# One 512-column pass of a split-precision gemm written as two passes of 256 columns

## The chip, the cores and the metric

The kernel runs on one NeuronCore of one Trainium2 chip. The metric is the device time of one execution in microseconds. A profile is one more execution, recorded by the hardware profiler.

## What is computed

Two transformer-like blocks run one after the other on one sequence of 256 tokens and a model width of 2048, all in float32. The first has a gated linear attention mixer, the second has a three-branch mixer (block attention, a gated linear recurrence, a short convolution). Each is followed by an MLP with a hidden width of 8192. Nearly all of the arithmetic is products of the activations with large weight matrices:

```
proj = h @ w_in                                   # both blocks
o = (o * silu(r)) @ w_out                         # block 1
x = x + square(relu(h @ w_up)) @ w_down           # MLP of each block
y = (g_a * y_a + g_b * y_b + g_c * y_c) @ w_out   # block 2
```

## The kernel before

All weights are read from HBM once, as a stream of units. A unit is 4 tiles of 128 rows by 256 columns of a weight matrix (512 KB in float32). SyncE's DMA queue loads it into one of four slots of `raw`.

A float32 number is held as two float32r numbers, a high and a low part. ScalarE writes the high part of a unit into `wsp[:, slot, t, 0]` (L746), and VectorE writes the low part into `wsp[:, slot, t, 1]` (L1003). The activations are held in the same way in `xs`, `hs`, `mixs` and `ycs`, with the high part at index 0 and the low part at index 1, each 256 tokens wide. The product of two such numbers is taken as high times high, plus high times low, plus low times high.

TensorE computes one block of 256 output columns with `gemm`. A block has up to four units, a unit has four tiles `t`, and a tile has two halves `j` of 128 columns. For each tile and half there are two passes over the array. The first has the high weights stationary and streams the high and the low activations, 512 columns (L472). The second has the low weights stationary and streams the high activations, 256 columns (L474). We call these two passes of one `(t, j)` a pair. The first pass writes `acc[:, g, j]`, whose half 0 collects high times high and whose half 1 collects the two cross products; the second pass adds to half 1. The two halves of one `j` are 512 float32 numbers of a partition, which fill one PSUM bank. `acc` has room for two blocks (`g`), and ScalarE (L755) and VectorE (L1011) take a finished block away while TensorE works on the next.

For two of the weight sections (`gv` and `v`) the roles are exchanged, so that tokens lie on the output partitions: the activations are stationary and the weights stream (`tokens_out`, L467 and L469). The pair has the same shape there.

The order of the work on each engine is written out by hand, and semaphores tie the engines together. TensorE waits for `lo_done` (the unit's low part is written) once in each unit, and for `split_done` (the activations are split) and `main_read` (the accumulator has been read). At the end of a unit it raises `unit_used`, which lets ScalarE overwrite the slot. The stream has 944 units, so there are 944 x 8 = 7552 pairs. The MLPs (`m1`, `m2`), the output projections (`go`, `lo`) and the mixer's third part (`mix`) run in hardware loops; the rest is written out straight. Between blocks of the straight part `hooks` and `hooks2` put small matmuls of the mixers on TensorE (attention scores at L572, L588 and others).

Every call of `pe.matmul` issues two instructions, a load of the stationary operand (LDWEIGHTS, in the profile on the row PEld) and the streaming pass (MATMUL, on the row PE).

Of the kernel before, what the change touches and what calls it, by code (L numbers as in the profile page):

```python
# [116 lines left out]
def build(nc, a, out, scratch):  # L117
# [3 lines left out]
    def at(name, shape, dt=F32, offset=None):  # L121
        size = -(-int(np.prod(shape[1:])) * 4 // 32) * 32
        if offset is None:
            offset = top[0]
            top[0] += size
        return nc.alloc_sbuf_tensor_at(name, shape, dt, offset=offset)
# [3 lines left out]
    wsp = at("wsp", [P, SLOTS, UK, 2, NB], F32R)  # L130
# [72 lines left out]
    def psum(name, shape):  # L203
        return ctx.enter_context(nc.psum_tensor(name, shape, F32))

    acc = psum("acc", [P, 2, 2, 2, T])
# [240 lines left out]
    def _(pe):  # L447
# [3 lines left out]
        def gemm(b, units, g, x, ready, k0=0, tokens_out=False, mid=None, before=None, mid_unit=2):  # L451

            if not (isinstance(b, int) and b < 2):
                pe.wait_ge(main_read, b - 1)
            for u, (rnd, slot) in enumerate(units):
                if before:
                    before(u)
                pe.wait_ge(lo_done, SLOTS * rnd + slot + 1)
                for s, v in ready(u):
                    pe.wait_ge(s, v)  # L460
                for t in range(UK):
                    k = UK * u + t
                    start, stop = k == 0, (u == len(units) - 1 and t == UK - 1)
                    for j in range(2):
                        cols = slice(j * P, j * P + P)
                        if tokens_out:
                            pe.matmul(acc[:, g, j], x[:, k0 + k, 0, cols], wsp[:, slot, t], start=start,  # L467
                                      stop=False, skip_group_check=True)
                            ins = pe.matmul(acc[:, g, j, 1], x[:, k0 + k, 1, cols], wsp[:, slot, t, 0],  # L469
                                            start=False, stop=stop, skip_group_check=True)  # L470
                        else:
                            pe.matmul(acc[:, g, j], wsp[:, slot, t, 0, cols], x[:, k0 + k], start=start,  # L472
                                      stop=False, skip_group_check=True)
                            ins = pe.matmul(acc[:, g, j, 1], wsp[:, slot, t, 1, cols], x[:, k0 + k, 0],  # L474
                                            start=False, stop=stop, skip_group_check=True)
                ins.then_inc(unit_used, 1)
                if mid and u == mid_unit:
                    mid()
# [125 lines left out]
        def straight(name, i, b, rnd, g):  # L604
            mid, before = (norm(0), inputs) if (name, i) == ("gk", 0) else (None, None)
            gemm(b, units_of(rnd, 0, 4), g, xs, split_upto(PAIR0["x1"]), tokens_out=(name == "gv"), mid=mid,
                 before=before, mid_unit=3)
            hooks(name, i)
# [3 lines left out]
        def out_proj(name, x, base):  # L612
            r0, b0 = ROUND0[name], BLOCK0[name]
            with pe.Fori(0, 4) as p:
                for g in range(2):
                    gemm(b0 + 2 * p + g, units_of(r0 + 2 * p + g, 0, 4), g, x, split_upto(base))
# [3 lines left out]
        def mlp(name, x_base, h_base, norm_no, final):  # L620
            def up(c, i, b, rnd, g, first=False):
                gemm(b, units_of(rnd, 0, 4), g, xs, split_upto(x_base),
                     mid=norm(norm_no) if first and g == 0 else None)

            def down(c, i, b, rnd, g, last=False):
                gemm(b, units_of(rnd, 0, 4), g, hs, split_upto(h_base + 8 * c))
                if last and final:
                    y_transpose(i)

            mlp_walk(loop, name, up, down)  # L630
# [86 lines left out]
        for j in range(TT):  # L717
            for k in range(2):
                ins = pe.matmul(M[0][:, 0, 2 * j:2 * j + 2], ssq[:, 0, k, j * P:(j + 1) * P], ones[:, 0:2], start=(k == 0),
                                stop=(k == 1), skip_group_check=True)  # L720
# [690 lines left out]
```

## Time and profile before

| what | value |
|---|---|
| time, median of 3 runs | 2806.29 us |
| lowest and highest run | 2803.33 and 2821.61 us |
| span of the profiled execution | 2804.5 us |
| mean granted TensorE clock | 0.989 |
| PE busy | 2770.4 us, 99% |
| DVE busy | 1797.0 us, 64% |
| ACT busy | 1353.2 us, 48% |
| DMA traffic | 504.47 MB, mean 180 GB/s |

The profiled execution lasted 2804.5 us from its first to its last instruction; the median of the runs is 1.8 us more. The ends of matmuls are modelled in the profile and neighbouring matmuls overlap in it, so a busy share of 99% says that passes follow one another without a break, and not how fast each is. How fast they are is read from their starts: the time from the start of one pass to the start of the next is called a slot below.

### The profile page before, as it was taken

How to read it: one execution, taken by the hardware profiler on the slowest of the kernel's cores; microseconds unless marked ns; L12 is line 12 of the kernel's file. 1: busy time of each engine (PE TensorE's matmuls, PEld its weight loads, DVE VectorE, ACT ScalarE, POOL GpSimd, SP SyncE). 2: the span in 40 equal slices, each digit the busy share in tenths (PEclk: the TensorE clock that was granted, in tenths of full speed). 3: DMA queues.
4: the chain of work that ended last, by engine and by line, in shares of the span. 5: the costliest groups of instructions: out<-in, count | busy, mean ns of one | idle time of the engine just before them, and what ended most of it. 6: DMA issues, size and time to landing. Idle time of an engine off the chain costs nothing.

```text
span 2804.5 us, 43839 instructions
## 1 busy us (share of the span) xinstructions
PE 2770.4 (99%) x15755; PEld 2401.9 (86%) x15755; DVE 1797.0 (64%) x2073; ACT 1353.2 (48%) x1632; POOL 86.3 (3%) x67
## 2 busy tenths in 40 slices
PE   8999999999999999999999999999999999999998
PEld 6888888888888888888888888888888888888887
DVE  6664677656656567765777666666676566565664
ACT  4543555444444445544575555554554444444443
POOL 3000001000000001300000000000000000000001
PEclk9998999999999999999999999999999999999999
DMA  6563455666666665665446556555556565565653
GB/s 182 157 201 89 136 187 187 193 189 186 193 190 185 191 191 185 193 210 173 150 151 195 181 181 191 189 183 188 184 182 191 185 186 185 182 187 189 185 186 128
DMA packets 507075, 504.47 MB, mean 180 GB/s; under 512 B 17731, under 2 KB 505432, under 8 KB 506984
## 3 DMA queue, kind: packets, MB, share of 16 engines
q1 hardware_dynamic: 505820, 501.60, 57.6%
q10 hardware_dynamic: 1164, 1.63, 0.2%
q8 instruction: 60, 0.98, 0.1%
q14 instruction: 31, 0.25, 0.0%
HBM read 499.50 MB, written 3.67 MB: 179 GB/s over the span
## 4 chain that ended last, share of the span: by engine, by line
PE 94%; DVE 3%; ACT 1%; issue 1%; POOL 0%; DVEq 0%; POOLq 0%; ACTq 0%
PE acc L472 57%; PE acc L474 29%; PE acc L467 3%; PE acc L469 2%; PE misc L588 1%; DVE wsp L1003 1%; DVE lat L1282 0%; PE misc L572 0%; ACT wsp L746 0%; PE misc L529 0%; PE misc L600 0%; DVE z L1011 0%; PE misc L692 0%; PE misc L488 0%; POOL ssq L434 0%
## 5 line engine op out<-in xcount | busy, mean ns | idle before, releaser
L1003 DVE TENSOR_TENSOR wsp<-raw,wsp 128x1024 fp32r<-128x1024 f32 x944 | 1167.6, 1244 | 624.8 <-ACT wsp L746 596.5
L472 PE MATMUL acc<-xs,wsp 128*128 128x512 f32 x4224 | 1496.7, 399 | 9.7 <-DVE wsp L1003 9.4
L746 ACT ACTIVATE wsp<-raw 128x1024 fp32r<-128x1024 f32 x944 | 992.4, 1056 | 736.3 <-PE acc L474 676.0
L474 PE MATMUL acc<-xs,wsp 128*128 128x256 f32 x4224 | 1183.5, 280 | 0.0
L472 PEld LDWEIGHTS acc<-xs,wsp 128*128 128x128 f32 x4224 | 797.1, 189 | 205.5 <-DVE wsp L1003 11.4
L472 PE MATMUL acc<-hs,wsp 128*128 128x512 f32 x2560 | 897.9, 396 | 0.0
L474 PEld LDWEIGHTS acc<-xs,wsp 128*128 128x128 f32 x4224 | 800.1, 189 | 0.7
L474 PE MATMUL acc<-hs,wsp 128*128 128x256 f32 x2560 | 714.1, 279 | 0.0
L472 PEld LDWEIGHTS acc<-hs,wsp 128*128 128x128 f32 x2560 | 480.5, 188 | 115.4
L474 PEld LDWEIGHTS acc<-hs,wsp 128*128 128x128 f32 x2560 | 482.2, 188 | 0.0
L755 ACT ACTIVATE corr<-acc 128x512 f32<-128x512 f32 x248 | 148.2, 598 | 417.7 <-PE acc L474 397.9
L1011 DVE TENSOR_TENSOR z<-acc,corr 128x512 f32<-128x512 f32 x248 | 171.5, 691 | 260.5 <-ACT corr L755 260.4
L434 POOL TENSOR_TENSOR ssq<-ssq,sq 128x512 f32<-128x512 f32 x48 | 74.8, 1564 | 2697.6 <-ACT sq L766 2016.8
L467 PE MATMUL acc<-wsp,xs 128*128 128x512 f32 x384 | 136.9, 401 | 0.0
L469 PE MATMUL acc<-wsp,xs 128*128 128x256 f32 x384 | 107.8, 281 | 0.0
L467 PEld LDWEIGHTS acc<-wsp,xs 128*128 128x128 f32 x384 | 72.1, 188 | 21.7 <-issue 4.1
L472 PE MATMUL acc<-mixs,wsp 128*128 128x512 f32 x256 | 90.5, 399 | 0.0
L760 ACT ACTIVATE hs<-z 128x512 f32 (+1 forms) x64 | 40.5, 633 | 91.2 <-DVE z L1201 91.2
L469 PEld LDWEIGHTS acc<-wsp,xs 128*128 128x128 f32 x384 | 72.5, 189 | 0.0
L474 PE MATMUL acc<-mixs,wsp 128*128 128x256 f32 x256 | 71.9, 281 | 0.0
L1180 DVE TENSOR_TENSOR xres<-xres,z 128x512 f32 (+1 forms) x80 | 55.4, 692 | 12.1 <-DVE z L1011 11.8
L472 PEld LDWEIGHTS acc<-mixs,wsp 128*128 128x128 f32 x256 | 48.1, 188 | 12.0
(208 smaller groups left out, 1076.8 us busy)
## 6 DMA issues: line engine op xcount, KB each, us to landing
raw<-in_w_in SPq DMA_DIRECT2D x224, 512.0 KB, 4.0
raw<-in_mlp_w_up SPq DMA_DIRECT2D x128, 512.0 KB, 4.0
raw<-in_mlp_w_down SPq DMA_DIRECT2D x128, 512.0 KB, 4.3
raw<-in_w_mlp_up SPq DMA_DIRECT2D x128, 512.0 KB, 4.0
raw<-in_w_mlp_down SPq DMA_DIRECT2D x128, 512.0 KB, 4.3
raw<-in_gla_w_in SPq DMA_DIRECT2D x96, 512.0 KB, 3.7
raw<-in_gla_w_out SPq DMA_DIRECT2D x32, 512.0 KB, 4.3
raw<-in_w_out SPq DMA_DIRECT2D x32, 512.0 KB, 4.0
```

Source lines behind the costliest of these rows:

```text
L434: ins = pool.tensor_tensor(ssq[:, k], ssq[:, k], sq[:, k], ALU.add)
L467: pe.matmul(acc[:, g, j], x[:, k0 + k, 0, cols], wsp[:, slot, t], start=start, stop=False, skip_group_check=True)
L469: ins = pe.matmul(acc[:, g, j, 1], x[:, k0 + k, 1, cols], wsp[:, slot, t, 0], start=False, stop=stop, skip_group_check=True)
L472: pe.matmul(acc[:, g, j], wsp[:, slot, t, 0, cols], x[:, k0 + k], start=start, stop=False, skip_group_check=True)
L474: ins = pe.matmul(acc[:, g, j, 1], wsp[:, slot, t, 1, cols], x[:, k0 + k, 0], start=False, stop=stop, skip_group_check=True)
L588: ins = pe.matmul(M[2 + dv // 2][:, dv % 2, cols], vtok[0:n, s, hd * DV + dv * P:hd * DV + (dv + 1) * P], scores_sb[0:n, hd % 2, s, cols], ...
L746: act.activation(wsp[:, slot, :, 0], raw[:, slot], ACT.Copy).then_inc(hi_done, 1)
L755: act.activation(corr[:, g], acc[:, g, :, 1], ACT.Copy).then_inc(corr_ready, 1)
L760: act.activation(pair(dst, i)[:, :, 0], src[:], ACT.Copy).then_inc(hi_ready, 1)
L1003: dve.tensor_tensor(wsp[:, slot, :, 1], raw[:, slot], wsp[:, slot, :, 0].bitcast(F32), ALU.subtract).then_inc(lo_done, 1)
L1011: dve.tensor_tensor(z[:], acc[:, g, :, 0], corr[:, g], ALU.add).then_inc(main_read, 1)
L1180: own.done(dve.tensor_tensor(pair(xres, i), pair(xres, i), z[:], ALU.add))
```

## The change

The 512-column pass of each pair becomes two passes of 256 columns. Both have the same stationary operand. The first streams the high activations into half 0 of the accumulator, and the second streams the low activations into half 1. The 256-column pass with the low weights stays. In the `tokens_out` form the same is done with the roles exchanged.

```diff
                         if tokens_out:
-                            pe.matmul(acc[:, g, j], x[:, k0 + k, 0, cols], wsp[:, slot, t], start=start,
+                            pe.matmul(acc[:, g, j, 0], x[:, k0 + k, 0, cols], wsp[:, slot, t, 0], start=start,
+                                      stop=False, skip_group_check=True)
+                            pe.matmul(acc[:, g, j, 1], x[:, k0 + k, 0, cols], wsp[:, slot, t, 1], start=False,
                                       stop=False, skip_group_check=True)
                             ins = pe.matmul(acc[:, g, j, 1], x[:, k0 + k, 1, cols], wsp[:, slot, t, 0],
                                             start=False, stop=stop, skip_group_check=True)
                         else:
-                            pe.matmul(acc[:, g, j], wsp[:, slot, t, 0, cols], x[:, k0 + k], start=start,
+                            pe.matmul(acc[:, g, j, 0], wsp[:, slot, t, 0, cols], x[:, k0 + k, 0], start=start,
+                                      stop=False, skip_group_check=True)
+                            pe.matmul(acc[:, g, j, 1], wsp[:, slot, t, 0, cols], x[:, k0 + k, 1], start=False,
                                       stop=False, skip_group_check=True)
                             ins = pe.matmul(acc[:, g, j, 1], wsp[:, slot, t, 1, cols], x[:, k0 + k, 0],
                                             start=False, stop=stop, skip_group_check=True)
```

## Rows read from the trace of the kernel before

**Rows 1.** The page: its first line, and the busy time of each engine.

```profile
span 2804.5 us, 43839 instructions
PE 2770.4 (99%) x15755; PEld 2401.9 (86%) x15755; DVE 1797.0 (64%) x2073; ACT 1353.2 (48%) x1632; POOL 86.3 (3%) x67
```

**Rows 2.** The page: the chain that ended last, by engine and by line.

```profile
PE 94%; DVE 3%; ACT 1%; issue 1%; POOL 0%; DVEq 0%; POOLq 0%; ACTq 0%
PE acc L472 57%; PE acc L474 29%; PE acc L467 3%; PE acc L469 2%; PE misc L588 1%; DVE wsp L1003 1%; DVE lat L1282 0%; PE misc L572 0%; ACT wsp L746 0%; PE misc L529 0%; PE misc L600 0%; DVE z L1011 0%; PE misc L692 0%; PE misc L488 0%; POOL ssq L434 0%
```

**Rows 3.** The page's costliest groups (line, engine; busy us, mean ns; idle before, releaser).

```profile
L1003 DVE TENSOR_TENSOR wsp<-raw,wsp 128x1024 fp32r<-128x1024 f32 x944 | 1167.6, 1244 | 624.8 <-ACT wsp L746 596.5
L472 PE MATMUL acc<-xs,wsp 128*128 128x512 f32 x4224 | 1496.7, 399 | 9.7 <-DVE wsp L1003 9.4
L746 ACT ACTIVATE wsp<-raw 128x1024 fp32r<-128x1024 f32 x944 | 992.4, 1056 | 736.3 <-PE acc L474 676.0
L474 PE MATMUL acc<-xs,wsp 128*128 128x256 f32 x4224 | 1183.5, 280 | 0.0
...
L474 PEld LDWEIGHTS acc<-xs,wsp 128*128 128x128 f32 x4224 | 800.1, 189 | 0.7
```

**Rows 4.** Windows by stage: us, busy us and instructions of each engine, clock, DMA share, GB/s.

```profile
14.00:320.00 306.00, 301.98 (x1691) 255.50 (x1692) 181.04 (x274) 141.42 (x184) 16.18 (x12) 0.93 0.49 143
320.00:1185.00 865.00, 864.86 (x4987) 756.09 (x4986) 573.12 (x602) 417.51 (x486) 41.59 (x26) 1.00 0.62 190
...
1480.00:2070.00 590.00, 590.00 (x3341) 511.64 (x3340) 381.82 (x408) 306.49 (x370) 11.43 (x8) 1.00 0.59 186
2070.00:2700.00 630.00, 630.00 (x3568) 546.32 (x3567) 389.19 (x399) 281.65 (x312) 0.95 (x1) 1.00 0.60 186
```

**Rows 5.** Timeline of PE in the first MLP (start us, length us).

```profile
899.61 0.40 PE L472 MATMUL acc<-xs,wsp 128*128 128x512 f32 x1
899.84 0.28 PE L474 MATMUL acc<-xs,wsp 128*128 128x256 f32 x1
899.96 0.39 PE L472 MATMUL acc<-xs,wsp 128*128 128x512 f32 x1
900.19 0.27 PE L474 MATMUL acc<-xs,wsp 128*128 128x256 f32 x1
900.30 0.40 PE L472 MATMUL acc<-xs,wsp 128*128 128x512 f32 x1
...
902.73 0.39 PE L472 MATMUL acc<-xs,wsp 128*128 128x512 f32 x1
```

**Rows 6.** Timeline of PE in the second MLP.

```profile
2299.65 0.40 PE L472 MATMUL acc<-xs,wsp 128*128 128x512 f32 x1
2299.89 0.28 PE L474 MATMUL acc<-xs,wsp 128*128 128x256 f32 x1
2300.01 0.40 PE L472 MATMUL acc<-xs,wsp 128*128 128x512 f32 x1
2300.25 0.28 PE L474 MATMUL acc<-xs,wsp 128*128 128x256 f32 x1
2300.36 0.40 PE L472 MATMUL acc<-xs,wsp 128*128 128x512 f32 x1
...
2302.83 0.40 PE L472 MATMUL acc<-xs,wsp 128*128 128x512 f32 x1
```

**Rows 7.** Timeline at 835 us, all engines, over the edge between two loop iterations.

```profile
835.36 0.28 PE L474 MATMUL acc<-xs,wsp 128*128 128x256 f32 x1
835.36 0.19 PEld L472 LDWEIGHTS acc<-xs,wsp 128*128 128x128 f32 x1
...
835.48 0.39 PE L472 MATMUL acc<-xs,wsp 128*128 128x512 f32 x1
835.48 0.19 PEld L474 LDWEIGHTS acc<-xs,wsp 128*128 128x128 f32 x1
```

**Rows 8.** Timeline of the first pairs of the kernel, before the clock rises.

```profile
14.85 0.63 PE L472 MATMUL acc<-xs,wsp 128*128 128x512 f32 x1
...
16.77 0.63 PE L472 MATMUL acc<-xs,wsp 128*128 128x512 f32 x1
```

**Rows 9.** Window of that stretch, columns as in the table by stage; the clock is 0.50.

```profile
14.50:17.00 2.50, 2.50 (x9) 2.11 (x9) 2.47 (x6) 1.59 (x3) 0.99 (x2) 0.50 0.62 96
```

**Rows 10.** Timeline at 215 us: small matmuls of 64 columns.

```profile
214.83 0.57 PE L572 MATMUL misc<-qT,keys_dec 128*64 128x64 f32 x7
```

## The prediction

> **What bounds the kernel now.** I read the busy times of the engines first. TensorE is busy for 99% of the span of 2804.5 us, the next engine for 64% [rows 1]. The chain of waits says the same in another way: 94% of it lies on PE, and 57% + 29% + 3% + 2% = 91% on the four lines of `gemm` [rows 2]. Third, the costliest groups. What the reader is to see there is who waits for whom: PE waited 9.7 us for the weights of L472 in all, while ScalarE waited 676.0 us for PE, and VectorE 596.5 us for ScalarE [rows 3]. So weights arrive and are split with time to spare, and the kernel is as long as TensorE takes for its 7552 pairs (944 units x 8), plus what the mixers put between them.
>
> The mean lengths of 399 ns and 280 ns [rows 3] are of no use for a sum, since the passes overlap. I take starts. The windows by stage give a pair's time where nothing else runs on PE, as the window over half its PE instructions: 865.00 / (4987 / 2) = 346.9 ns in the first MLP, 590.00 / 1670.5 = 353.2 ns in the mixer's third part, 630.00 / 1784 = 353.1 ns in the second MLP [rows 4]. Weighted by their lengths, 351 ns. The timelines divide a pair: in the first MLP nine pairs take 902.73 - 899.61 = 3.12 us, each slot that begins with a 512-column pass is 0.23 us, so the nine 256-column slots share 1.05 us, 117 ns each [rows 5]. In the second MLP nine pairs take 3.18 us, nine wide slots of 0.24 us make 2.16, and the narrow ones are 1.02 / 9 = 113 ns [rows 6]. Starts are rounded to 10 ns there, so these means are good to some 2 ns. Together, eighteen narrow slots are 115 ns, eighteen wide ones 235 ns: the narrow slot is half the wide one, within the reading. The same code runs at two slightly different paces in the two MLPs, which the trace doesn't explain.
>
> **The change, part by part.** (1) Columns. The work streamed is the same: 256 + 256 + 256 instead of 512 + 256, into the same bank, in the same order. (2) The wide slot goes and two narrow ones come. The nearest row for a narrow float32r pass is the narrow pass that is there already: it follows another pass on the same half of the accumulator, it has a weight load beside it, and it is 113 to 117 ns long. Another reading is half of the wide slot, 235 / 2 = 117.5 ns. I take 116 ns, between 115 (its own slot) and 117.5. A pair becomes 3 x 116 = 348 ns against 350 (115 + 235), that is -2 ns, and 7552 x -2 ns = -15 us. (3) One more weight load for each pair, 7552 in all, of weights that are in the array already. In the trace every matmul has its own load, 15755 of each [rows 1], so I count none as left out. A load's record starts with the pass before the one it serves, at 835.36 and again at 835.48 [rows 7]: the load for L472 lies beside the narrow pass of L474, and is done when that pass's slot of 0.12 us is over. So a load fits under a 256-column pass now, and with three narrow passes each load has such a cover. Cost zero in my sum. If the cover were short by the spread of narrow slots (113 to 117, so 4 ns), it would be 4 x 7552 = 30 us. (4) 15104 more instructions for PE's sequencer, three loads and three passes in 350 ns, or 58 ns an instruction. Seven matmuls of 64 columns with their loads take 0.57 us, of which the last is 0.22: six steps of 58 ns, each a load and a pass [rows 10]. That is 29 ns an instruction, half of what is needed. Cost zero. At the edge between two loop iterations the slot is 0.12 us like any other [rows 7], though the sequencer has its branch to do there; with shorter instructions it is ahead by a third less in time. There are some 76 such edges, and if each showed one slot of 0.12 us, that is 9 us. (5) ScalarE, VectorE, the loads from HBM and all semaphores keep their place: `unit_used` is raised by the same last pass, and the DMA share of 0.6 [rows 4] leaves room at any pace within 5% of this one.
>
> Sum: 2804.5 - 15 = 2790 us of span, and with the 1.8 us to the median 2791 us. Within 1% of before is 2778 to 2834 (about what a measurement of this kernel can tell from no change).
>
> The Trainium skill, TensorE: Matmul & The Clock Gate, section The mechanism (of Part 3), states that a weight load overlaps with a matmul under way only when it is for another row group. Here all passes use all rows, so by that rule every load would stand between two passes. The trace speaks against it: load and pass start together, and a pair with two loads takes 347 to 353 ns [rows 4, 7]. The Trainium skill, same page, section Back-to-back issue gap, gives a spacing of N/2.4 + 2.5 ns for one matmul after another. By it a pair would go from 325 to 327.5 ns, and the change would cost, as an estimate from that page, 2.5 x 7552 = 19 us; the measured pair is 22 to 28 ns longer than its 325.
>
> **The rivals.** *A pass has a price of its own (slower).* At the start, with the granted clock at 0.50 (1.2 GHz), three pairs take 16.77 - 14.85 = 1.92 us, 640 ns each, which is exactly 768 columns at 1.2 GHz, with nothing over [rows 8, 9]. At the full clock 768 columns at 2.4 GHz are 320 ns, but the pair takes 346.9 to 353.2 [rows 4]. Something of 27 to 33 ns appears only at the higher clock. My forecast has it proportional to columns (stalls of the stream). If it belongs instead to the two passes, or their two weight loads, then each costs 13.5 to 16.6 ns, and a third costs as much again: 7552 x 13.5 to 16.6 = +102 to +125 us, so 2908 to 2931 us. It decides as soon as more than half of the excess is tied to the pass. For it: the excess comes in once the stream is twice as fast, when a handover between passes of a fixed length would no longer be hidden. Against it: equal shares would give slots of 213 + 15 = 228 and 107 + 15 = 122 ns, and the trace has 230 to 240 and 113 to 117 [rows 5, 6]. Only my reading of starts speaks here, and where a start is recorded need not be where the array begins. The Trainium skill, on the same page and in the section Back-to-back issue gap, has a rule of that kind: the spacing is set by load and pass together, 81 ns at 128 columns and 131 ns at 512. The figures are not those of this trace, where 512 columns take 230 to 240 ns.
>
> *The wide pass alone carries the excess (faster).* The wide slot has 230 to 240 where 213 would do, so 17 to 27 ns too much; the narrow one has 6 to 10 too much [rows 5, 6]. If a narrow pass can hold its shortest value, 113 ns [rows 6], whatever precedes it, the pair is 339 ns, and 7552 x (339 - 351) = -91 us, which gives 2716 us; with half of the pairs doing so, 2760 us. For it: a regular train of equal passes may settle into one pace, as the two MLPs show that pace isn't fixed by the code. Against it: in the first MLP the narrow slot is 117 ns, and there the pair as a whole is the faster one.
>
> *The sequencer or the load becomes the bound (slower).* A train of loads without the long cover of a wide pass could slip by more than I allow: with narrow slots of 120 ns (the upper of the two values that the timelines print) a pair is 360 ns, 7552 x 9 ns = +68 us, 2874 us. For it: many single slots read 0.12. Against it: they alternate with 0.11 [rows 5].
>
> *The change does nothing to the array* (the second load is dropped somewhere, because the weights are the same): then two passes stream 512 columns as before, and the time stays at 2806 us; this can't be told from my forecast by the time, only by the count of loads.
>
> **How the numbers follow.** Forecast with the last case: 0.50, at 2791 us, its own range 2770 to 2830. A price for each pass: 0.25, 2908 to 2931. Narrow slots at their longest: 0.08, about 2874. Faster narrow slots: 0.17, 2716 to 2760. Of the forecast's 0.50 I put 0.07 below 2778 and 0.04 above 2834. So faster by over 1%: 0.17 + 0.07 = 0.24; slower by over 1%: 0.25 + 0.08 + 0.04 = 0.37; within 1%: 0.39. Both signs are open, and the range reaches to both: from 2735 (leaving out the lower part of the fast case, some 0.08) to 2918 (leaving out the upper half of the case of a price for each pass, some 0.12).
>
> **What the changed profile would show.** PE and PEld would have 15755 + 7552 = 23307 instructions each; fewer loads would mean the last case. ScalarE would still wait some 676 us for PE, and PE hardly for VectorE; if not, (5) is wrong. The window of a stage over a third of its PE instructions is the slot: 116 ns by my forecast, 120 to 123 if each pass has a price, 113 if the wide pass was the costly one. A slot longer at loop edges alone would put the fault in (4). At the clock of 0.50 a pair should still take 640 ns in every case; more there would mean a price that the higher clock doesn't bring. The prediction is wrong if the recorded starts hide where the 27 to 33 ns belong, for everything hangs on that one division of a pair.

## The result and the profile after

The changed kernel takes 2883.28 us (median of 4 runs, 2881.69 to 2885.29) against 2804.81 us for the kernel before (median of the 3 runs of before and one more). The ratio of these medians is 1.0280. The ratio on record is 1.0333, with a 95% interval of 1.0285 to 1.0382; it is not the ratio of these eight runs alone. The kernel before was also timed beside the experiments, with medians of 2804.36 us (13 runs) and 2783.45 us (17 runs). So the change costs some 3%, 2.8% to 3.6% by what it is held against. The forecast was 2791 us, no change within 1%.

The page of the changed kernel, its first line, busy times, instruction queue and chain (the lines of `gemm` are now L474, L476 and L478 for the three passes, L467, L469 and L471 in the `tokens_out` form):

```profile
span 2883.2 us, 58943 instructions
PE 2844.4 (99%) x23307; PEld 2822.7 (98%) x23307; DVE 1798.6 (62%) x2073; ACT 1354.0 (47%) x1632; POOL 86.3 (3%) x67
...
q8 instruction: 113, 1.85, 0.3%
...
PE 94%; DVE 3%; ACT 1%; issue 1%; POOL 0%; DVEq 0%; POOLq 0%; ACTq 0%
PE acc L474 29%; PE acc L476 29%; PE acc L478 29%; PE acc L467 2%; PE acc L471 2%; PE acc L469 2%; PE misc L592 1%; DVE wsp L1007 1%; DVE lat L1286 0%; DVE z L1015 0%; PE misc L576 0%; ACT wsp L750 0%; PE misc L533 0%; PE misc L604 0%; PE misc L492 0%
...
L750 ACT ACTIVATE wsp<-raw 128x1024 fp32r<-128x1024 f32 x944 | 992.8, 1055 | 795.9 <-PE acc L478 727.1
L474 PE MATMUL acc<-xs,wsp 128*128 128x256 f32 x4224 | 1207.6, 286 | 16.4 <-issue 9.1
```

Answers to [rows 1 to 3]. PE and PEld have 23307 instructions each, 7552 more, so no load was dropped. DVE and ACT do the same work in the same time (1798.6 and 1354.0 us), ScalarE still waits for PE (727.1 us), and the chain still runs on PE. The kernel is longer because PE is slower at the same columns. The timeline of PE in the first MLP shows how:

```profile
899.84 0.28 PE L474 MATMUL acc<-xs,wsp 128*128 128x256 f32 x1
899.96 0.28 PE L476 MATMUL acc<-xs,wsp 128*128 128x256 f32 x1
900.08 0.28 PE L478 MATMUL acc<-xs,wsp 128*128 128x256 f32 x1
...
901.64 0.28 PE L474 MATMUL acc<-xs,wsp 128*128 128x256 f32 x1
```

Fifteen slots take 901.64 - 899.84 = 1.80 us, 120 ns each, and every start is 0.12 us after the last. There is no alternation of 0.11 and 0.12 any more [rows 5]. Windows inside the two MLPs (us, busy us and count, clock, DMA share, GB/s), of the changed kernel:

```profile
500.00:1100.00 600.00, 600.00 (x5002) 1.00 0.58 183
2150.00:2650.00 500.00, 500.00 (x4169) 1.00 0.58 185
```

and of the kernel before:

```profile
500.00:1100.00 600.00, 600.00 (x3464) 1.00 0.61 190
2150.00:2650.00 500.00, 500.00 (x2832) 1.00 0.60 186
```

A pair, now of three passes, is 600 / (5002 / 3) = 359.9 ns and 500 / (4169 / 3) = 359.8 ns after, where it was 346.4 and 353.1 ns. The unrounded starts of the traces say 360.0 in both, and 346.7 and 353.3 before. So the two paces of the kernel before are one now, and slower than either: 13.3 ns more for a pair in the first MLP, 6.7 ns in the second.

A second, smaller part is in the loop of the mixer's third part. The timeline of the changed kernel at 1710 us:

```profile
1710.04 0.28 PE L478 MATMUL acc<-ycs,wsp 128*128 128x256 f32 x1
...
1712.81 0.19 PEld L474 LDWEIGHTS acc<-xs,wsp 128*128 128x128 f32 x1 [2.70 <-issue]
1712.82 0.42 PE L474 MATMUL acc<-xs,wsp 128*128 128x256 f32 x1 [2.50 <-issue]
```

From the start of the last pass of an iteration to the start of the first of the next there are 2.78 us, and PE is released by nothing that the profile shows ("issue"). At the two other edges of that loop it is 3.81 and 3.31 us, 9.9 us in all. The kernel before has none of these gaps. After each gap the granted clock is 0.50 for a stretch, and the passes there take 0.21 us each. The loop as a whole, first in the kernel before and then in the changed one, and a stretch after the first gap:

```profile
1564.93:1971.97 407.04, 407.04 (x2306) 1.00 0.59 186
...
1606.48:2035.46 428.98, 419.92 (x3459) 0.99 0.55 178
1713.00:1716.00 3.00, 3.00 (x15) 0.50 0.29 97
```

The loop is 21.9 us longer. 1152 pairs of 360.0 ns would take 414.7 us, 7.7 more than before; the other 14.3 us come with the gaps. The standing still makes 9.9 - 3 x 0.12 = 9.5 us of them and the passes at the low clock the rest, some 4.7 us. The instruction queue moved 113 packets, against 60 before.

The ledger, by the starts at the edges of the stages: `go` and `m1` (2304 pairs) are 30.7 us longer, which is 13.3 ns a pair; `lo` and `m2` (2304 pairs) 15.3 us, which is 6.7 ns a pair; the loop of the third part 21.9 us; the straight parts of the two mixers, where pairs ran at both paces before and small matmuls lie between them, 3.9 and 6.8 us. Together 78.6, and the spans differ by 2883.2 - 2804.5 = 78.7 us. So the pairs cost 64 us and the gaps 14.

### The profile page after: what moved, and what is told of

Its sections match the earlier page's. It is cut to its first block, busy times and chain, and to the rows that moved or that the text cites. A ratio compares the mean times of both kernels' runs of the same rounds, so it can differ in the third digit from the quotient of the medians.

```text
span 2883.2 us, 58943 instructions
## 1 busy us (share of the span) xinstructions
PE 2844.4 (99%) x23307; PEld 2822.7 (98%) x23307; DVE 1798.6 (62%) x2073; ACT 1354.0 (47%) x1632; POOL 86.3 (3%) x67
## 4 chain that ended last, share of the span: by engine, by line
PE 94%; DVE 3%; ACT 1%; issue 1%; POOL 0%; DVEq 0%; POOLq 0%; ACTq 0%
PE acc L474 29%; PE acc L476 29%; PE acc L478 29%; PE acc L467 2%; PE acc L471 2%; PE acc L469 2%; PE misc L592 1%; DVE wsp L1007 1%; DVE lat L1286 0%; DVE z L1015 0%; PE misc L576 0%; ACT wsp L750 0%; PE misc L533 0%; PE misc L604 0%; PE misc L492 0%
## 5 line engine op out<-in xcount | busy, mean ns | idle before, releaser
L750 ACT ACTIVATE wsp<-raw 128x1024 fp32r<-128x1024 f32 x944 | 992.8, 1055 | 795.9 <-PE acc L478 727.1
L474 PE MATMUL acc<-xs,wsp 128*128 128x256 f32 x4224 | 1207.6, 286 | 16.4 <-issue 9.1
L476 PE MATMUL acc<-xs,wsp 128*128 128x256 f32 x4224 | 1201.8, 285 | 0.0
L478 PE MATMUL acc<-xs,wsp 128*128 128x256 f32 x4224 | 1201.3, 284 | 0.0
L474 PEld LDWEIGHTS acc<-xs,wsp 128*128 128x128 f32 x4224 | 817.7, 194 | 19.8 <-issue 10.5
L476 PEld LDWEIGHTS acc<-xs,wsp 128*128 128x128 f32 x4224 | 817.7, 194 | 0.7
L478 PEld LDWEIGHTS acc<-xs,wsp 128*128 128x128 f32 x4224 | 817.6, 194 | 0.0
L474 PE MATMUL acc<-hs,wsp 128*128 128x256 f32 x2560 | 724.9, 283 | 0.0
L478 PE MATMUL acc<-hs,wsp 128*128 128x256 f32 x2560 | 724.5, 283 | 0.0
L476 PE MATMUL acc<-hs,wsp 128*128 128x256 f32 x2560 | 724.5, 283 | 0.0
L474 PEld LDWEIGHTS acc<-hs,wsp 128*128 128x128 f32 x2560 | 491.5, 192 | 0.0
L476 PEld LDWEIGHTS acc<-hs,wsp 128*128 128x128 f32 x2560 | 491.5, 192 | 0.0
L478 PEld LDWEIGHTS acc<-hs,wsp 128*128 128x128 f32 x2560 | 491.5, 192 | 0.0
L759 ACT ACTIVATE corr<-acc 128x512 f32<-128x512 f32 x248 | 148.0, 597 | 435.2 <-PE acc L478 414.7
L467 PE MATMUL acc<-wsp,xs 128*128 128x256 f32 x384 | 109.5, 285 | 0.0
L471 PE MATMUL acc<-wsp,xs 128*128 128x256 f32 x384 | 108.7, 283 | 0.0
L469 PE MATMUL acc<-wsp,xs 128*128 128x256 f32 x384 | 108.7, 283 | 0.0
L467 PEld LDWEIGHTS acc<-wsp,xs 128*128 128x128 f32 x384 | 73.7, 192 | 4.1 <-issue 4.1
```

The source lines that it names most:

```text
L467: pe.matmul(acc[:, g, j, 0], x[:, k0 + k, 0, cols], wsp[:, slot, t, 0], start=start, stop=False, skip_group_check=True)
L469: pe.matmul(acc[:, g, j, 1], x[:, k0 + k, 0, cols], wsp[:, slot, t, 1], start=False, stop=False, skip_group_check=True)
L474: pe.matmul(acc[:, g, j, 0], wsp[:, slot, t, 0, cols], x[:, k0 + k, 0], start=start, stop=False, skip_group_check=True)
L476: pe.matmul(acc[:, g, j, 1], wsp[:, slot, t, 0, cols], x[:, k0 + k, 1], start=False, stop=False, skip_group_check=True)
L750: act.activation(wsp[:, slot, :, 0], raw[:, slot], ACT.Copy).then_inc(hi_done, 1)
L759: act.activation(corr[:, g], acc[:, g, :, 1], ACT.Copy).then_inc(corr_ready, 1)
```

## The experiments

Three theories were open on the slots: the price is fixed for each pass and its load (A); it is the load's, in proportion to its columns (B); narrow passes wait for a load of 120 ns and the wide pass has an excess of its own (C). A fourth was that the gaps are a matter of the instruction supply of that loop.

**Trains of equal passes.** The kernel has ScalarE cast one tile and then issues only matmuls; one train of it, with N = 48:

```diff
+        for i in range(N):
+            pe.matmul(acc[:, i % 4, 0:384], w[:, i % 8], x[:, 0:384], **flags(i))
```

> This kernel leaves out the whole computation and issues only trains of 48 equal matmuls on TensorE, one train after the other, with ScalarE, VectorE and the DMA queues idle. Each source line is one train, so the slot is read off for each kind of pass. Theory A, each pass (or its weight load) costs 13.3 ns over its columns at 2.4 GHz: float32r passes of 512, 384, 320 and 256 columns have slots of 226.7, 173.3, 146.7 and 120.0 ns. Theory B, the excess belongs to the load and shrinks with it: with 64 columns of stationary operand in place of 128 the slots are 220 and 113.3 ns, and with 32 they are 216.7 ns at 512. Theory C, a narrow pass waits for a load of 120 ns, and a wide pass has an excess in its stream: 512 columns take 230 to 235 ns, 384 columns about 173 to 177, 256 columns 120. Repeating the same stationary operand changes nothing in A, B and C; if a load of what is already there were free, the slots would fall to 107 to 109 and 213 to 216 ns. bfloat16 trains tell whether the excess is one of float32r.

Timeline of PE in that kernel, one row a train; the time from a train's start to the next one's, over 48, is its slot:

```profile
19.64 11.04 PE L61 MATMUL acc<-x,w 128*128 128x512 f32 x48
30.52 8.51 PE L63 MATMUL acc<-x,w 128*128 128x384 f32 x48
38.87 7.19 PE L65 MATMUL acc<-x,w 128*128 128x320 f32 x48
45.90 5.92 PE L67 MATMUL acc<-x,w 128*128 128x256 f32 x48
51.66 5.92 PE L69 MATMUL acc<-x,w 128*128 128x256 f32 x48
57.42 11.07 PE L71 MATMUL acc<-x,w 128*128 128x512 f32 x48
68.32 11.20 PE L73 MATMUL acc<-x,w 128*64 128x512 f32 x48
79.36 5.61 PE L75 MATMUL acc<-x,w 128*64 128x256 f32 x48
...
95.93 10.53 PE L79 MATMUL acc<-xb,wb 128*128 128x512 bf16 x48
106.30 5.40 PE L81 MATMUL acc<-xb,wb 128*128 128x256 bf16 x48
111.46 0.48 PE L84 MATMUL acc<-x,w 128*128 128x512 f32 x1
```

512 columns: (30.52 - 19.64) / 48 = 226.7 ns. 384 columns: 8.35 / 48 = 174. 320: 7.03 / 48 = 146.5. 256: 5.76 / 48 = 120.0. By the single starts in the second half of each train they are 226.7, 173.3, 146.7 and 120.0: the columns at 2.4 GHz plus 13.3 ns, whatever the width, as theory A had it for 128 stationary columns. Theory C falls: the wide pass among wide ones has 226.7, not 230 to 235. L69 and L71 load the same weights every time and are no faster (120.0 and 227). A train that writes one accumulator bank all along has 120.0 as well.

With fewer stationary columns no theory holds. With 64 of them 256 columns take 113.3 ns, as B had it and A had not, but 512 take 230, which A and B both miss, and with 32 they take 231.6 where B had 216.7. In bfloat16 the slots are 215.8 and 109.2 ns (again by the second half), 2.5 ns over the columns: the price of 13.3 is one of float32r. The Trainium skill, TensorE: Matmul & The Clock Gate, section Back-to-back issue gap, has N/2.4 + 2.5 ns; these bfloat16 trains agree to 0.1 ns, and the float32r trains have 13.3 in place of its 2.5.

**The second trains: smaller loads, and how a pace comes about.**

> This kernel leaves out the whole computation; again it issues only trains of 48 passes, one source line each. The first trains gave 13.3 ns over the columns for each float32r pass with 128 stationary columns at any width, 6.7 ns with 64 stationary columns at a width of 256, but 16.8 and 18.4 ns with 64 and 32 stationary columns at a width of 512. Theory B' (the price is that of the load, in proportion to its columns): at a width of 256 the excess is 13.3, 10, 6.7 and 3.3 ns for 128, 96, 64 and 32 stationary columns, slots 120, 116.7, 113.3 and 110.0. Theory A' (a fixed price of a pass, with exceptions): no such line. At 384 columns B' gives 170, 166.7 and 163.3 ns. Then four trains of alternating 512 and 256 columns, each after another lead-in (none, three short bfloat16 passes, three float32 matmuls, three float32r passes of 384 columns). If the pace of 346.7 or 353.3 ns for a pair is chosen by the moment at which the train begins, the four differ; if it belongs to the code or the place, all four have 353.3, as the one alternating train in the first run. The train wide, wide, narrow, narrow should have 693.3 to 697 ns for four passes.

```profile
20.05 5.92 PE L62 MATMUL acc<-x,w 128*128 128x256 f32 x48
25.80 5.73 PE L64 MATMUL acc<-x,w 128*96 128x256 f32 x48
31.36 5.61 PE L66 MATMUL acc<-x,w 128*64 128x256 f32 x48
36.81 5.61 PE L68 MATMUL acc<-x,w 128*32 128x256 f32 x48
42.26 8.56 PE L70 MATMUL acc<-x,w 128*96 128x384 f32 x48
50.65 8.48 PE L72 MATMUL acc<-x,w 128*64 128x384 f32 x48
58.97 8.48 PE L74 MATMUL acc<-x,w 128*32 128x384 f32 x48
67.30 10.52 PE L76 MATMUL acc<-raw 128*128 128x256 f32 x48
```

At 256 columns, 128, 96, 64 and 32 stationary columns give 120.0, 116, 113.3 and 113.3 ns; the last should have been 110.0 by B'. At 384 columns 96, 64 and 32 stationary columns give 175, 173.4 and 173.3 ns, as with 128. So a load of a quarter of the columns costs as much as a whole one there, and B' falls; at 256 columns there is a part of some 7 ns that a smaller load saves. Plain float32 (L76) has 215.8 ns for 256 columns, 2.5 ns over two cycles a column. Its train has 24 calls and 48 passes: a float32 `pe.matmul` issues two loads and two passes, where the float32r and bfloat16 ones issue one of each. So the price shows in a float32r stream at the full clock. Every pass of these kernels has a load of its own, so whether the 13.3 ns are the pass's or the load's can't be told from them; the 7 ns speak for a share of the load.

The alternating train of the first kernel, 21 pairs between these two rows:

```profile
111.89 0.40 PE L84 MATMUL acc<-x,w 128*128 128x512 f32 x1
...
119.31 0.40 PE L84 MATMUL acc<-x,w 128*128 128x512 f32 x1
```

and the first one of this kernel, 12 pairs:

```profile
78.00 0.40 PE L78 MATMUL acc<-x,w 128*128 128x512 f32 x1
...
82.16 0.40 PE L78 MATMUL acc<-x,w 128*128 128x512 f32 x1
```

7.42 / 21 = 353.3 ns a pair there, 4.16 / 12 = 346.7 ns here, and all four alternating trains here have 346.6 to 346.8 by their starts. The same passes with the same operands run at either pace. Neither branch of the expectation came true: the four don't differ, and they don't have 353.3. The two kernels ran on two chips, and what comes before the train differs too; but the kernel before has both paces in one execution, so neither the chip nor the data alone chooses. What chooses stays open. It doesn't take the surroundings of the mixer, for here all other engines are idle. The train wide, wide, narrow, narrow took 697.5 ns for its four passes, at the upper end of 693.3 to 697.

**Half of the split.** Against the kernel before, only pairs with `j == 1` are split. In place of the wide pass of either form there is now this (an excerpt; `hi[0]` and `hi[1]` are both its stationary operand, `mv` is its moving one):

```diff
+                        if j == 1:
+                            for s in range(2):
+                                pe.matmul(acc[:, g, j, s], hi[s], mv[:, s], start=(start and s == 0), stop=False,
+                                          skip_group_check=True)
+                        else:
+                            pe.matmul(acc[:, g, j], hi[0], mv, start=start, stop=False, skip_group_check=True)
```

> Only the pairs of the second half (j = 1) have their 512-column pass split; 3776 passes are added in place of 7552. Theory A (13.3 ns for each pass): four halves of two tiles follow one another with 5 passes and 1536 columns for two pairs, 640 + 5 x 13.3 = 706.7 ns against 693.3 to 706.7 before and 720 with all split, so about 2825 to 2835 us, halfway. Theory C (load floor of 120 ns in narrow slots, excess in the wide stream): wide 231 to 236, then four narrow slots at 113 to 120, 693 to 716 ns, the same or a little less than A. If the price were one of the regular train (all passes equal), this kernel would stay at the time of before, 2805 us.

It took 2837.61 us, 3 us above the expected range, ratio 1.0124 (1.0056 to 1.0193). The windows of this kernel:

```profile
500.00:1100.00 600.00, 600.00 (x4221) 1.00 0.61 184
2150.00:2650.00 500.00, 500.00 (x3518) 1.00 0.61 185
```

Five passes take 600 / (4221 / 5) = 710.7 ns, where 640 + 5 x 13.3 is 706.7. So A is right to 4 ns in a mixed order, and the price doesn't need a regular train. This run doesn't tell A from C, which allowed 693 to 716 ns; the trains do. The loop of the third part shows no gap here, with 1440 loads and passes in its body (1152 before, 1728 after).

**Neighbours with other weights.** The six passes of a tile in another order, so that the same weights never follow one another. The passes are written as a list of kind and half; "0" and "1" are the two parts of the split pass, and in this writing the changed kernel has ("0", 0), ("1", 0), ("low", 0), ("0", 1), ("1", 1), ("low", 1). The line of the new order alone:

```diff
+                    order = (("0", 0), ("0", 1), ("1", 0), ("1", 1), ("low", 0), ("low", 1))
```

> The changed kernel with the order of the six passes of a tile altered, so that no two neighbouring passes have the same stationary operand: high times high of both halves, then high times low of both, then low times high of both. Theory A or B (13.3 ns for every load and pass, whatever was loaded before): slots of 120.0 ns and 2883 us, as the changed kernel. If a load of weights that are already there were cheaper, this one would be slower than the changed kernel; if writing the same half of the accumulator twice in a row cost anything, this one would be faster.

2882.72 us (2880.45 to 2885.42), ratio 1.0335 (1.0283 to 1.0387), and slots of 120.00 ns by the starts: nothing changed, and the three gaps of the loop are there too. That the added load is of weights already in the array neither helps nor hurts, and neither does writing the same half of the accumulator twice in a row.

**Where the gaps come from.** One kernel splits everywhere but in the loop of the third part, the other only there (`if in_mix`). Against the half split:

```diff
-                        if j == 1:
+                        if not in_mix:
```

> All passes are split as in the changed kernel, except the 1152 pairs of the third part of the mixer (the loop of four iterations with 36 units each), which stay 512 + 256. In the changed kernel this loop showed three gaps of 2.8, 3.8 and 3.3 us at its iteration edges, that the kernel before hadn't, and more instruction DMA (113 packets against 60). Theory: the loop body had become too long for the instruction buffer and is fetched again. Then the gaps are gone here and the instruction packets return to some 60 to 75; the time is 2883 - 10 (gaps, less a passing slow clock after each) - 1152 x 7 ns = 8, so about 2865 us. Rival: the gaps come from a wait on another engine at that place, and stay.

> The kernel before, with only the 1152 pairs of the mixer's third part split. Theory: 1152 x (360 - 353.3) = 8 us for the passes and 10 us for three gaps of about 3 us at the edges of that loop's iterations, 2804 + 18 = 2822 us; the number of instruction packets rises from 60 to about 100. If the gaps came from the whole program's size and not from this loop's body, there would be none.

Outside only: 2863.42 us, ratio 1.0216 (1.0147 to 1.0286), no gap at that loop, 84 instruction packets where 60 to 75 were expected. Its loop takes 407.04 us, as in the kernel before. Inside only: 2833.15 us (2819.56 to 2839.89), ratio 1.0155 (1.0098 to 1.0212), 89 packets, and gaps of 3.5, 2.4 and 3.9 us at the same three edges. That is 11 us above the expected 2822, in runs that spread over 20; the profiled spans differ by 2826.3 - 2804.5 = 21.8 us, as the 21.9 us of the loop in the ledger. The window in the loop with the gaps:

```profile
1500.00:2000.00 500.00, 491.05 (x3861) 0.99 0.56 180
```

So the gaps need this loop's body to be long, and not the whole program. The packets say how. The split outside the loop adds two instructions to each of 3072 pairs of the program's text and 84 - 60 = 24 packets, so a packet holds 256 instructions. The split inside adds only 2 x 288 = 576 instructions to the text, some 2 packets, but there are 89 - 60 = 29 more. Where the other 27 are is seen in the DMA view of the last three iterations: from 1700 to 2035 us of the changed kernel there are 27 instruction packets, and from 1690 to 1999 us of the half split, in the same loop, none; the view lists the data queue alone. Below, these two and then the view of the first gap, from 1709.70 to 1712.82 us:

```profile
q8 instruction: 27, 0.44, 0.6%
...
q1 hardware_dynamic: 57759, 57.37, 58.5%
...
q8 instruction: 1, 0.02, 2.4%
```

The split inside only has 27 in its last three iterations, too. So the long body is fetched again in each iteration, 9 packets each time, and the shorter one is not. And each of the nine gaps of the three kernels that have them (changed, other weights, inside only) has one instruction packet under way at its start; this packet takes 1.0 to 3.1 us, and PE starts again 1.5 to 1.8 us after its end, in gaps of 2.4 to 3.9 us. That PE waits for these instructions is what the nine agree on; the wait itself is in no record.

**Two other orders without the split**, to see if the price can be had for less. The first has the passes of a tile as wide, wide, narrow, narrow; the second has the eight wide ones of a unit, then the eight narrow ones.

Written as above, the kernel before has ("wide", 0), ("low", 0), ("wide", 1), ("low", 1). The line of the first, and the outer loop of the second around that of the tiles (excerpts):

```diff
+                    order = (("wide", 0), ("wide", 1), ("low", 0), ("low", 1))
...
+                for wide in (True, False):
+                    for t in range(UK):
```

> The kernel before, with the same passes, but the order in a tile is both wide passes (j = 0 and 1), then both narrow ones. Theory A (13.3 ns a pass, whatever the order): the pair keeps 346.7 ns in the better of its two paces, 693.3 ns for a tile; if the slower pace (353.3) doesn't arise, 2783 us, otherwise as before, 2805. Theory C: a narrow slot after a narrow one is 120 ns and a wide slot 231 to 236, so 2 x 351 to 356 ns, 2805 to 2845 us.

> The kernel before with its passes in the order: the eight wide ones of a unit, then the eight narrow ones. By the first trains a wide pass among wide ones has a slot of 226.7 ns and a narrow one among narrow ones 120.0, 346.7 ns for the two, which is the better pace of the kernel before (346.7 or 353.3) and a little less than in the order wide, wide, narrow, narrow (348.4). So 7552 x (346.7 - 350.9) = -32 us against the profiled 2804.5, that is 2775 to 2783 us, and runs that agree with one another, where the kernel before spreads from 2780 to 2823. Rival: the changeovers between widths cost more than I think, or the wide passes lock into 233 ns also here; then 2790 to 2805 us.

The windows of the first MLP, of wide, wide, narrow, narrow:

```profile
500.00:1100.00 600.00, 600.00 (x3447) 1.00 0.61 188
```

and of the order by unit:

```profile
500.00:1100.00 600.00, 600.00 (x3439) 1.00 0.60 188
```

600 / (3447 / 2) = 348.1 ns a pair, and 348.9. Both hold this pace through the whole kernel, in both MLPs, and their runs agree with one another: 2785.0 to 2790.96 us (10 runs) and 2791.89 to 2797.52 us (12 runs). The kernel before had 2780.48 to 2808.48 us and once 2822.84 beside the first (median of the 13 is 2804.36), and 2774.18 to 2814.15 us beside the second (median 2783.45). The ratios are 0.9974 (0.9943 to 1.0005) and 1.0022 (0.9994 to 1.0051). So neither is shown to beat the kernel before; both lie within its spread, and only hold their time better. In the first order the pair missed the 346.7 ns of A by 1.6 (348.3 by the starts) and lay below the 351 to 356 of C. By unit the wide slots were 230.1 ns by the starts and not 226.7 as in the train, so that expectation missed by 12 us, and its rival (2790 to 2805 us) came in.

## Why the prediction was wrong

**What bounds the kernel** was right: PE's passes, before and after, with every other engine waiting. **Step (5)** held: ScalarE still waits for PE. **Step (3)** held in that no load is left out, 23307 of each, and in that nothing changes when the loads' neighbours do. That the load fits under its pass at no cost was not shown by its row: the load's record is 0.19 us long [rows 7], longer than the slot of 0.12 us that I said it was done in. And the trains leave open how much of the 13.3 ns is the load's. The low clock showed what I had said. The timeline of PE in the changed kernel at the start, and its window, with the clock of 0.50:

```profile
15.05 0.41 PE L474 MATMUL acc<-xs,wsp 128*128 128x256 f32 x1
...
16.98 0.41 PE L474 MATMUL acc<-xs,wsp 128*128 128x256 f32 x1
...
14.50:17.00 2.50, 2.50 (x13) 2.50 (x14) 2.46 (x6) 1.39 (x3) 0.98 (x2) 0.50 0.43 63
```

Nine passes in 1.93 us are 643 ns for the three of a pair, and before it was 640 ns for its two [rows 8]: no price of a pass there, within the rounding.

**Step (2) failed**, and with it the sum. I took 116 ns for a narrow pass, from what its neighbours left it in the trace, and it is 120.0 ns when all passes are narrow. A pair went to 3 x 120.0 = 360.0 ns and not to 348: 13.3 or 6.7 ns more than before in place of 2 less, and 64 us for all pairs in place of -15.

The readings behind it were worse than I said, too. I called them good to 2 ns, but starts rounded to 10 ns repeat the same error in every pair. By the unrounded starts over the windows above, the narrow slot is 115.0 ns and the wide one 231.7 in the first MLP (I had 117 and 230), 117.0 and 236.3 in the second (113 and 240). Still, better readings would not have shown the 120.

The half-to-whole ratio of the slots (115 to 235 ns) made me hold the excess of 27 to 33 ns for a matter of columns. The trains show that it is 13.3 ns for each float32r pass with 128 stationary columns, at 256, 320, 384 and 512 columns alike: 2 x 13.3 + 320 = 346.7 is the better pace of before to the tenth, and 3 x 13.3 + 320 = 360.0 is the pace after. How the excess is spread over a wide and a narrow slot in the recorded starts of a mixed order says nothing of whose it is. That was the last sentence of my prediction, and I should have given it more weight: the cold stretch, 640 ns exactly, was in the rows, and a stall in proportion to columns gives no reason why it should vanish there. A handover of fixed length that is hidden under the slower stream would; no run shows the handover itself.

**The rivals.** The price for each pass was the right mechanism, mis-sized: I gave every pass half of 27 to 33 ns and came to 2908 to 2931 us, but the other 6.7 ns of the slower pace are no price of a pass; they vanish in the regular train. The rival with narrow slots at their longest had the slot right, 120 ns, and 68 us for the pairs where 64 were measured; with the 14 us of the gaps, which it didn't have, it would be at 2888. I had given it 0.08. That it came so near is in part luck: it put the 120 ns down to the sequencer or the load as a bound, and a bound of that kind would have left wide passes alone. The fast rival fell with the trains: a wide pass among wide ones carries 13.3 ns like any other, and the narrow slot of 113 ns that it stood on was the rounding.

**Step (4) failed in its second part.** The sequencer keeps up inside the loops and at the edges of the MLP loops, where slots stay at 120 ns. But I put its cost at zero, with 9 us for 76 edges as the worst, and 14 us came from three edges of one long loop. I had looked at how far the sequencer is ahead, and not at how long the loop bodies become. My sign for this fault, a slot longer at loop edges alone, is what the trace has there.

## What to carry to other kernels

Where float32r passes stream at full rate, count passes and not only columns: a train of equal passes, or two widths of it, gives the fixed part of each, and a division of an alternating pattern by its recorded starts does not. Look whether an excess is there at the lower clock as well: here it was not, which spoke against a stall in proportion to columns. Don't average rounded starts of a pattern that repeats. And when a change lengthens the body of a hardware loop, look at the instruction packets and at the edges of the longest loop.

## What the runs showed of the hardware

- A float32r pass with 128 stationary columns costs 13.3 ns over its columns at the full clock (226.7, 173.3, 146.7 and 120.0 ns for 512, 384, 320 and 256), a bfloat16 pass 2.5 ns (215.8 and 109.2), a float32 pass 2.5 ns over two cycles a column (215.8 for 256; a float32 `pe.matmul` issues two). No run parts the pass from its load. With 64 stationary columns a float32r pass takes 113.3 ns for 256 columns and 230 for 512. At a granted clock of 0.50 the float32r pass has no excess.
- The same alternation of wide and narrow float32r passes runs at 346.7 or 353.3 ns a pair, at both in one execution of the kernel before and at either with all other engines idle, and keeps its pace for hundreds of us. If executions differ in how long they keep each pace, that would account for the 40 us by which runs of the kernel before differ (6.7 ns x 7552 = 50 us), where the split one's differ by 4; this is argued, not shown. What chooses the pace is open.
- With 1728 loads and passes in the body of a hardware loop, its instructions were fetched again in each iteration, in 9 packets of 256, and PE stopped for 2.4 to 3.9 us at each iteration edge. With the granted clock of 0.50 after each stop, the three edges cost 14 us in the changed kernel. With 1440 there was no instruction packet in the later iterations and no stop.
